# A decoder layer with 32 experts: weights in thirds of 48 KB a partition, chunks fetched ahead for experts 14 to 17, and smaller pooling matrices widened by ScalarE

## The reference

```python
n = rms_norm(h, norm1_w)
q, k, v, u = split(n @ w_in)                  # 8 query heads, 2 key/value heads, width 64; u: 512 wide
q, k = partial_rope(rms_norm(q)), partial_rope(rms_norm(k))
attn_out = sliding_window_attention(q, k, v, sinks)     # window 128
# pooling: 4 groups of 128 columns, means over the last 2, 4, 8, 16 tokens, less the token itself
pool_out = einsum('bsgc,gcd->bsgd', pooled, pool_w) * pool_scale
h = h + concat(attn_out, pool_out) @ w_out
n2 = rms_norm(h, norm2_w)
# mixture of experts: the top 4 of 32 for each token, weighed by a softmax
gu = n2[toks] @ w_gu[e] + b_gu[e]             # 1024 x 2048 for each expert
act = min(gate, 7) * sigmoid(1.702 * gate) * (clip(up, -7, 7) + 1)
y = act @ w_down[e] + b_down[e]               # 1024 x 1024 for each expert
h = h + sum over the chosen experts of gate * y
```

## Time and profile before

| | |
|---|---|
| median of 3 runs | 988.99 us (988.66 to 989.54) |
| the profiled execution | 988.7 us |
| its span, first to last instruction | 986.9 us |
| TensorE busy | 96% |
| moved by DMA | 418.27 MB, 424 GB/s over the span |
| load queue (q1), share of 16 engines | 99.2% |
| mean granted TensorE clock | 0.987 |

### The profile page before, as it was taken

One profiled execution on the slowest core, in us unless ns is written; L12 is line 12 of the kernel. 1 busy time (PEld: TensorE's weight loads), 2 busy tenths in 40 slices (PEclk: granted clock), 3 DMA queues, 4 the chain that ended last, 5 costly groups with the idle time before them and its releaser, 6 DMA issues.

```text
span 986.9 us, 11112 instructions
## 1 busy us (share of the span) xinstructions
PE 946.6 (96%) x4508; PEld 382.4 (39%) x4508; DVE 202.9 (21%) x610; ACT 127.7 (13%) x346; POOL 14.0 (1%) x9
## 2 busy tenths in 40 slices
PE   9999999999999899898989989889989999999997
PEld 5545433333333334333333333333333333333432
DVE  4645121212111121210112121011212112111121
ACT  2433111011110111010011101001101110011101
POOL 0031000000000000000000000000000000000000
PEclk9999999999999999999999999999999999999999
DMA  9999999999999999999999999999999999999996
GB/s 374 426 423 398 412 429 434 432 430 428 432 431 429 436 430 430 434 432 429 434 433 426 437 432 428 437 430 429 436 429 431 432 429 430 431 433 430 422 422 272
DMA packets 23869, 418.27 MB, mean 424 GB/s; under 512 B 2912, under 2 KB 3296, under 8 KB 8224
## 3 DMA queue, kind: packets, MB, share of 16 engines
q1 hardware_dynamic: 23408, 417.20, 99.2%
q10 hardware_dynamic: 432, 0.66, 0.2%
HBM read 416.80 MB, written 1.05 MB: 423 GB/s over the span
## 4 chain that ended last, share of the span: by engine, by line
PE 63%; DMA 36%; DVE 1%; issue 0%; ACT 0%; SPq 0%; DVEq 0%
DMA ring<-w_gu_dram 33%; PE ps L1237 29%; PE ps L1342 14%; PE ps L1205 4%; PE ps L1189 4%; DMA ring<-w_down_dram 3%; PE ps L1066 3%; PE ps L997 2%; PE ps L1004 1%; PE ps L1293 1%; PE ps L1301 1%; PE ps L1013 0%; PE ps L1039 0%; PE ps L1058 0%; PE ps L1046 0%
## 5 line engine op out<-in xcount | busy, mean ns | idle before, releaser
L1237 PE MATMUL ps<-ring,passing 128*64 128x512 f32 x1008 | 229.1, 604 | 14.8 <-DMA ring<-w_gu_dram 14.8
L1237 PE MATMUL ps<-ring,PR 128*64 128x512 f32 x976 | 224.5, 608 | 16.4 <-DMA ring<-w_gu_dram 16.2
L1342 PE MATMUL ps<-ring,PT 128*64 128x512 f32 x984 | 218.3, 595 | 0.5 <-DMA ring<-w_down_dram 0.5
L952 DVE TENSOR_SCALAR xw<-ps 128x256 f32<-128x256 f32 x64 | 27.2, 425 | 650.0 <-PE ps L1237 650.0
L1237 PEld LDWEIGHTS ps<-ring,passing 128*64 128x64 f32 x1008 | 76.8, 139 | 158.3 <-issue 143.8
L1237 PEld LDWEIGHTS ps<-ring,PR 128*64 128x64 f32 x976 | 74.9, 140 | 157.0 <-issue 145.4
L1342 PEld LDWEIGHTS ps<-ring,PT 128*64 128x64 f32 x984 | 68.1, 137 | 129.6 <-issue 127.5
L652 ACT ACTIVATE xw<-xw 128x256 f32<-128x256 f32 x64 | 26.6, 416 | 484.5 <-DVE xw L952 484.5
L1205 PE MATMUL ps<-PT 64*128 64x512 f32 x248 | 69.7, 640 | 0.0
L1189 PEld LDWEIGHTS ps<-qk,X 128*128 128x128 f32 x512 | 59.6, 191 | 18.8 <-issue 18.8
L1189 PE MATMUL ps<-qk,X 128*128 128x128 f32 x512 | 65.7, 281 | 0.0
(11 more groups left out here) (198 smaller groups left out, 374.6 us busy)
## 6 DMA issues: line engine op xcount, KB each, us to landing
ring<-w_gu_dram SPq DMA_DIRECT2D x48, 4096.0 KB, 28.2
ring<-w_down_dram SPq DMA_DIRECT2D x25, 4096.0 KB, 29.7
ring<-w_gu_dram SPq DMA_DIRECT2D x14, 2048.0 KB, 14.2
ring<-w_gu_dram SPq DMA_DIRECT2D x6, 3072.0 KB, 23.2
ring<-w_down_dram SPq DMA_DIRECT2D x5, 2048.0 KB, 23.1
ring<-w_gu_dram SPq DMA_DIRECT2D x9, 1024.0 KB, 9.6
ring<-w_down_dram SPq DMA_DIRECT2D x8, 1024.0 KB, 25.9
ring<-w_down_dram SPq DMA_DIRECT2D x2, 3584.0 KB, 27.6
```

The source lines that it names most:

```text
L952: nc.vector.tensor_scalar(gb[:, b, :], gu[:, b, 0, :], LIMIT, None, ALU.min).then_inc(g_ready, 1)
L1237: last = mm(ps[64 * j:64 * j + 64, GU + b, :], lhs, halves[j][:, 512 * b:512 * b + 512], start=start, stop=stop)
L1342: last = mm(ps[64 * j:64 * j + 64, bank, :], at[:, k, 64 * (c - GU_PIECES):64 * (c - GU_PIECES) + 64], rows[:, 512 * j:512 * j + 512], sta ...
```

## The change

- The expert weights lie in one array, `w_all`, in halves of an expert: 48 KB a partition (6 MB, three pieces). The ring has nine slots in place of eight; `extra` is gone.
- The first 30 pieces are loaded mostly one by one (before: 22), then halves of an expert by `load_part` up to part 52, then pieces one by one again for expert 26's second half up to expert 29. The last two experts keep their order and cuts, but the last row comes in two column halves.
- The chunks fetched ahead are the first 1 MB of experts 14 to 17 and 1 MB of expert 14's second half.
- The pooling matrices are loaded as 180 KB in place of 544 KB: 144 columns of each group in bfloat16, which holds their values exactly, and its first 16 columns in float32. ScalarE widens and places them with four copies between `qkv_out(0)` and `qkv_out(1)`.
- The last result is copied and added in two halves of 256 columns.
- TensorE's experts 0 to 29 are straight code (`expert(e, ...)` called with a number), and SP's loads too; ScalarE and VectorE keep their loops. The product with the down biases moves from behind expert 3 to behind expert 5.

```diff
-RING = 8
+RING = 9
-PAIR = 2 * PIECE
+PART = 3
+TRIPLE = PART * PIECE
+SLOTS_OF = RING // PART
+FIRST_PLACE = (NE - 2) * PIECES
-BY_CHUNK, SINGLES = (RING, RING + 1, RING + 3), 14
+BY_CHUNK, SINGLES = (RING, RING + 1, RING + 3), 21
+LATE = 2 * (NE - 6) + 1
-            (2, 4): ((0, 2), (2, 4), (4, 6), (6, 7), (7, 8)), (3, 4): ((0, 2), (2, 4), (4, 6), (6, 7), (7, 8))}
+            (NE - 2, 4): ((0, 2), (2, 4), (4, 6), (6, 7), (7, 8)), (NE - 1, 4): ((0, 2), (2, 4), (4, 6), (6, 7))}
+LAST_COLUMNS = ((0, 256), (256, 512))
-AHEAD = 6
+AHEAD, AHEAD_FROM = 4, 14
...
-        extra = sb("extra", [P, 4, 1024])
...
-            sp.dma_start(band, bands.rearrange("p (g s) -> p g s", g=NG)).then_inc(ld_bands, 16)
-            sp.dma_start(poolw, w_pool.rearrange("p (g n) -> p g n", g=NG)).then_inc(ld_bands, 16)
+            sp.dma_start(packed, bands).then_inc(ld_bands, 16)
+            sp.dma_start(poolw, w_pool.rearrange("p (g n) -> p g n", g=NG)).then_inc(ld_poolw, 16)
...
-            load_pair(0)
+            load_piece(0, stop=2 * PIECE)
             load_piece(RING + 2)
-            for n in range(8, 2 * AHEAD):
-                load_ahead(n)
+            load_piece(RING - 1)
...
-            for s in range(RING + SINGLES, RING + 2 + TP, 2):
-                sp.wait_ge(pieces_used, s + 2 - RING)
-                load_pair(s)
-            with sp.Fori(1, TURNS - 3) as r:
-                for s in range(RING + 2, RING + 2 + TP, 2):
-                    sp.wait_ge(pieces_used, r * TP + s + 2 - RING)
-                    load_pair(s, r * TURN)
...
+            first_part = (RING + SINGLES) // PART
+            for part in range(first_part, LATE):
+                sp.wait_ge(pieces_used, PART * (part + 1) - RING)
+                begun = 0 <= part // 2 - AHEAD_FROM < AHEAD and part % 2 == 0 or part == 2 * AHEAD_FROM + 1
+                load_part(part, 2 * FF if begun else 0)
+            for s in range(PART * LATE, FIRST_PLACE):
+                sp.wait_ge(pieces_used, s + 1 - RING)
+                load_piece(s, done=landed_late[s % RING])
...
+                if (e, first_c) == (NE - 1, GU_PIECES):
...
+                    for q, (a, b) in enumerate(LAST_COLUMNS):
+                        sp.dma_start(ends[:, :, a:b], rows[:, :, a:b]).then_inc(landed_cols[q], 16)
...
             qkv_out(0)
+            act.wait_ge(ld_bands, 16)
+            for dst, src in ((band[:, :, EDGE:REACH], exact[:, :, 0:P]), (band[:, :, REACH + EDGE:REACH + P], exact[:, :, 0:P - EDGE]),
+                             (band[:, :, REACH:REACH + EDGE], exact[:, :, P:P + EDGE]), (band[:, :, 0:EDGE], edge)):
+                nc.scalar.copy(dst, src).then_inc(unpacked, 1)
             qkv_out(1)
...
-            down_out(NE - 1, 0, GU + 1, ye_last)
+            act.wait_ge(pieces_used, NE * PIECES)
+            for done, (a, b) in zip((y_first, y_sb), LAST_COLUMNS):
+                nc.scalar.copy(ye_last[:, a:b], ps[:, GU + 1, a:b]).then_inc(done, 1)
...
-            pe.wait_ge(ld_bands, 32)
+            pe.wait_ge(unpacked, 4)
...
-            with pe.Fori(1, TURNS - 2) as r:
-                for u in range(TURN):
-                    expert(r, u)
-            for u in range(TURN):
-                expert(TURNS - 2, u, early=u)
...
+            expert(0, "first")
             pe.wait_ge(GdT_sb, 1)
...
+            for e in range(1, NE - 2):
+                expert(e, early=e - AHEAD_FROM if 0 <= e - AHEAD_FROM < AHEAD else None)
+                if e == TURN + 1:
+                    pe.wait_ge(ld_bdn, 16)
...
-            pe.wait_ge(y_sb, NE)
             for t in range(T):
-                for last in to_tokens(t, GT_last, ye_last):
-                    last.then_inc(acc_final, 1)
+                for q, (a, b) in enumerate(LAST_COLUMNS):
+                    pe.wait_ge(*((y_first, 1), (y_sb, NE))[q])
```

More of the change, by code:

```diff
@@ L47 @@
 REACH = P + max(POOLS)
+EDGE = max(POOLS)
+PACKED = NG * (P + EDGE) // 2 + NG * EDGE
 NE, TOPK, FF = 32, 4, 1024
@@ L392, in _ @@
             sp.dma_start(bias[:, :, :].rearrange("p t n -> p (t n)"), b_gu).then_inc(ld_bgu, 16)
[L394 to L409, removed]
+            def load(part, slot, first=0, stop=TRIPLE, at=None):
+                at = slot * TRIPLE + first if at is None else at
+                dst = ring[:, at:at + stop - first].rearrange("p (o n) -> p o n", o=1)
+                return sp.dma_start(dst, w_k[:, bass.ds(part, 1), first:stop])
@@ L411, in load_ahead, with load_piece, load_part @@
+            def load_piece(s, first=0, stop=PIECE, done=None):
+                part, base = s // PART, s % PART * PIECE
+                load(part, part % SLOTS_OF, base + first, base + stop).then_inc(done or landed[part % SLOTS_OF], 16)
+            def load_part(part, skip):
+                load(part, part % SLOTS_OF, skip).then_inc(landed[part % SLOTS_OF], 16)
             def load_ahead(n):
-                src = w_gu_k[:, (NE - 2 * TURN + n // 2) * 2, 0:2 * FF]
-                sp.dma_start(ahead[n], src[:, n % 2 * FF:(n % 2 + 1) * FF]).then_inc(ld_ahead[n // 2], 16)
@@ L486, in _ @@
-            for n in range(0, 2 * PIECES, 2):
[L487 to L497, removed]
+            first_part = (RING + SINGLES) // PART
@@ new lines, in _, with place_of @@
+            for part in range(first_part, LATE):
[5 more added lines that the diff above has]
+                load_piece(s, done=landed_late[s % RING])
+            for n in range(0, 2 * PIECES, 2):
+                e, first_c = LAST_TWO[n]
+                sp.wait_ge(pieces_used, FIRST_PLACE + n + 2 - RING)
+                per, wide = (4, DM) if first_c >= GU_PIECES else (2, 2 * FF)
+                def place_of(k):
+                    c = k // per + (GU_PIECES if first_c >= GU_PIECES else 0)
+                    slot = (FIRST_PLACE + LAST_TWO.index((e, c))) % RING
+                    return 2 * e + c // PART, c % PART * PIECE + k % per * wide, slot * PIECE + k % per * wide
+                for k, stop in END_CUTS[e, first_c]:
+                    part, first, at = place_of(k)
+                    load(part, 0, first, first + (stop - k) * wide, at).then_inc(landed_end[e, first_c, k], 16)
+                if (e, first_c) == (NE - 1, GU_PIECES):
+                    part, first, at = place_of(KC - 1)
+                    ends = ring[:, at:at + DM].rearrange("p (j n) -> p j n", j=2)
+                    rows = w_k[:, part, first:first + DM].rearrange("p (j n) -> p j n", j=2)
+                    for q, (a, b) in enumerate(LAST_COLUMNS):
+                        sp.dma_start(ends[:, :, a:b], rows[:, :, a:b]).then_inc(landed_cols[q], 16)
@@ L499, in next_pass @@
             def next_pass(p, r):
-                for s in range(0, TP, 2):
-                    sp.wait_ge(pieces_used, p * (NE * PIECES) + r * TP + (s + 2 - RING))
-                    load_pair(s, r * TURN)
+                for u in range(TURN):
+                    for h in range(2):
+                        sp.wait_ge(pieces_used, p * (NE * PIECES) + r * TP + u * PIECES)
+                        load(r * (2 * TURN) + 2 * u + h, h).then_inc(landed_more[h], 16)
             more_passes(sp, TURNS, next_pass)
@@ L1099, in _ @@
             attend(0)
+            pe.wait_ge(ld_poolw, 16)
             for g in range(NG):
@@ L1367, in expert @@
                 down()
[L1369 to L1387 removed]
+            expert(0, "first")
+            pe.wait_ge(GdT_sb, 1)
+            for e in range(1, NE - 2):
+                expert(e, early=e - AHEAD_FROM if 0 <= e - AHEAD_FROM < AHEAD else None)
+                if e == TURN + 1:
+                    pe.wait_ge(ld_bdn, 16)
+                    for t in range(T):
+                        for c in range(2):
+                            mm(ps[:, ACC[t] + c, :], GdT[c * NE:(c + 1) * NE, t, :], bdn[c * NE:(c + 1) * NE, :], start=False, stop=True, skip_group_check=True)
+            gate_up, between, _, _, down = expert(NE - 2, "last but one")
             gate_up()
             between()
[L1390 removed]
+            gate_up, _, turn_round, turn_gates, down_last = expert(NE - 1, "last")
             gate_up()
@@ L1402, in _ @@
             pe.wait_ge(gt_sb, NE)
-            pe.wait_ge(y_sb, NE)
             for t in range(T):
-                for last in to_tokens(t, GT_last, ye_last):
-                    last.then_inc(acc_final, 1)
+                for q, (a, b) in enumerate(LAST_COLUMNS):
+                    pe.wait_ge(*((y_first, 1), (y_sb, NE))[q])
+                    for j in range(2):
+                        last = mm(ps[:, ACC[t] + j, a:b], GT_last[64 * j:64 * j + 64, t, :], ye_last[64 * j:64 * j + 64, a:b],
+                                  start=False, stop=True, skip_group_check=True)
+                        if b == 512:
+                            last.then_inc(acc_final, 1)
             def next_pass(p, r):
                 for u in range(TURN):
-                    expert(p * TURNS + r, u, "more")
+                    expert(u, "more", later=p * TURNS + r)
```

154 lines of the change are left out of this document (77 added, 77 removed).

## The result

The changed kernel takes 992.95 us (median of 9 runs, 991.19 to 994.96) against 989.3 us (9 runs, 988.66 to 989.54): a ratio of 1.0037, interval 1.0028 to 1.0045. It is 3.65 us slower, where +1.1 was forecast, and 0.35 us above the range. The profiled execution is the longest of its nine: 994.96 us, span 993.1, so some 2 us of what it shows are its own.

What follows compares the result with a forecast made beforehand. The prediction took a DMA load queue that never runs dry, plus start and tail, as the bound. Bands -0.87, thirds -0.5, packets +0.2, last columns -0.2 and fetches +2.5 made +1.1 us: 990.1 us, range 986.8 to 992.6.

Steps and rivals of the forecast that it cites:

- Bands of 180 KB: -0.87 us: Front: loading 364 KB less of pooling matrices puts every later load 0.87 us ahead; ScalarE's widening is hidden at no cost.
- it holds by 0.8: Load issued at 118.5 us: the queue's reserve is 1.7 us, the smaller bands take 0.87, so it stays fed.
- If the share falls below 1.0 between 100 and 130 us: Sign in the profile after that would prove the prediction wrong; DMA share was expected at 1.0 up to 960 us.
- 16 x 0.16 = 2.5 us: TensorE's unrolled program: about 16 more instruction fetches of 16 KB on the DMA engines, 0.16 us each, +2.5 us; bound +5.
- in the stalled middle a period of 58.5: Two experts' period expected at 58.5 us; at or below 58.2 would mean fetches free, above 58.7 fetches on the last engine.
- Thirds and pieces: -0.5: Weight loads: 131 in place of 141 for the same bytes, at most -0.7 us, taken as -0.5.
- The ring of three thirds: Middle: asked whether it starves the load queue; claimed the queue stays fed, the next third having 13.5 us to go.
- The last columns: -0.2: Tail: the last row in column halves saves some 0.5 us of products, wider final products add 0.25; between -0.6 and +0.2.
- with 0.2 back for packets: Last row's halves: 1 KB rows mean 24 more packets an engine, +0.2 us if a load's 0.07 us lies in its packets.
- Fetches cost nothing: Rival: fetches fall on engines that aren't last, so only the -1.4 us remains, 987.6 us; chance 0.22.
- Fetches fall on the last engine: Rival: 16 fetches cost 3.8 to 5.0 us, giving 991.4 to 992.6 us; chance 0.20.
- the queue runs dry: Rival, also covering slower 48 KB rows: late widening or third's release costs 1 to 3 us more, 991.1 to 993.1; chance 0.08.

## Why the prediction was wrong

Two steps failed: the term of the bands, put at -0.87 us, of which nothing shows in the changed kernel, and the size of the fetches, 2.5 us where 3.1 were measured. Together they are 1.5 us of the 2.55 by which +1.1 missed +3.65.

**"Bands of 180 KB: -0.87 us ... it holds by 0.8."** This step failed. The widening is hidden, as said (26.89 us), and up to 115 us every load is 0.9 us ahead. But the load issued at 118.5 us is released by TensorE at its own time, and loads ahead by 0.87 us find the queue empty on more of the engines. I had measured the reserve there from the engine that was last: 1.7 us. The average engine had 0.3 and the first none. In the profiles, 0.35 of the 0.87 us at most stays in the queue behind it for the bands alone (by the medians 0.6), and in the changed kernel nothing; there the medians agree: 992.95 with small bands, 992.64 with whole ones. "If the share falls below 1.0 between 100 and 130 us" was named as a sign that the prediction is wrong: it is 0.99 at 384 GB/s in the profiled run, and 403 GB/s against 419 at full clock.

**"16 x 0.16 = 2.5 us."** Right in kind and the largest term, too small in size: the straight code alone measured 3.1 us (1.9 to 4.4) for 17 fetches, 0.18 us each, where I had 0.16 and 16. The mean hides the mechanism. A fetch makes one engine 1.5 us late for good, and a landing waits for the last engine, so it costs nothing or far more: 0.73 us in a period of the straight code, 1.5 in one of the changed kernel. My bounds took a fetch at the price of its bytes, 0.04 us spread evenly and 0.61 on the last engine; the runs show 0.10 (1.54 / 16) and 1.5. That 0.16 from ten mixed fetches came near 0.18 is partly luck. My step "in the stalled middle a period of 58.5" spread the cost evenly and was wrong as a test: periods of 58.13 with fetches in them fall on the side that I had named for "fetches free", and the time was lost in other periods. The Trainium skill, "Runtime: NRT & Kernel Launch", section "Instruction fetch mechanics", calls the cost of crossing a block mostly hidden; here the measurement decides against it, by these 3.1 us.

**"Thirds and pieces: -0.5."** The price a load is right (0.05 to 0.075 us, from 32 loads more), and ten loads fewer are -0.5 to -0.7 by it. No run has the thirds alone. Straight code with the changed front, thirds and halves, at whole bands, is at 992.64 and straight code alone at 992.29, so the gain doesn't show in the medians. The ring of three thirds starved nothing in the middle (58.13).

**"The last columns: -0.2", with 0.2 back for packets.** The span gave 0.1 back, the executions nothing: alone +0.6 us by the medians, with an interval from -0.2 to +1.6, and 0.7 of it outside the span. In the changed kernel they are within the noise (992.95 against 992.44 without).

**The sum.** +3.1 - 0.7 for the thirds is +2.4, with bands and halves at nothing; measured +3.65 (2.8 to 4.5). The kernel with whole bands is at +3.4 (2.1 to 4.6). So some 1.2 us more is not accounted for by the medians; the intervals just allow it. A likely source is the fall of the clock near 90 us with the starved stretch behind it, which cost the queue 1.2 and 1.7 us in the two profiles that have it. They are the longest executions of their kernels (994.96 and 996.59 us). The two of the changed front without it are the shortest of theirs (991.56 and 991.33), close to 989.3 + 2.4 = 991.7. But these are four executions, and one fetch that fell on the last engine has its share in the longest; that the clock carries the medians is not shown, nor is what makes it fall.

**The rivals.** "Fetches cost nothing" is refuted. "Fetches fall on the last engine" (0.20) and "the queue runs dry" (0.08) both happened in part, the first in some periods, the second between 115 and 137 us. I treated them as alternatives, and so no case had both; either's upper end was near 993.

## What to carry to other kernels

Where the DMA engines are the bound, count the instruction fetches: here a loop of four experts that stays in place fetched nothing for 460 us, while straight code paid for each block with 1.5 us on one engine, and the landing waits for the last engine. Bytes saved early pay only while the queue stays deep up to the next bottleneck. Look for its emptiest moment over a whole stretch, and measure the reserve from the first engine to run out, not from the landing, which is the last one's. When two executions are compared, the mean of a load's 16 parts shows the work done, and the last part adds which engine was late. And before a change is built on a ring of nine pieces, see what the ring asks of the code: here slots repeat after three experts and the pairs' buffers after four, so a loop's body would be twelve experts long.

## What the runs showed of the hardware that was not expected

- 17 rows of 16 KB in one transfer went to a single DMA engine, one behind the other (10.7 us a transfer), 16 rows of 17 KB to all (0.6 us); a single row of 16 KB is cut in 16 by itself.
- A 16 KB fetch of instructions makes one DMA engine 1.5 us late and leaves the other 15 as they were; a 16 KB row of weights takes 0.61 us.
- Where nothing is fetched, the lag between the first and the last DMA engine doesn't shrink while the queue is full: 2.45 us at 303 us and 2.47 at 767, with every load passing through both.
- The granted clock fell to half for 3.4 us in the middle of unbroken work of TensorE (7.67 of 8 us busy before), in two of the three profiles with the changed front and small bands, and in none of the eleven others.
- With column halves of the last row, all 22 executions of the two kernels with TensorE's loop lie 2.2 to 3.2 us above their spans; those of the changed kernel lie 1.8 to 1.9 above, like the rest.
- The last store's issue took SP 0.47 us in the kernel with bands and halves and 1.70 in the changed one, for the same 256 KB.
